# RMSNorm statistics of a two-layer encoder step: plain fp32 averaging and square root with reciprocal, in place of split sums and Ln with Exp

## What is computed

```python
def rms_norm(x, g):
    xf = x.astype(jnp.float32)
    y = xf * lax.rsqrt(jnp.mean(xf * xf, axis=-1, keepdims=True) + EPS)
    return (y * g.astype(jnp.float32)).astype(x.dtype)

for l in range(DEPTH):                                   # DEPTH = 2
    h = rms_norm(xp, ln_mix[l])                          # then projections, attention, x += o @ w_out
    ...
    xp = xp + cross_attend(rms_norm(xp, ln_mem[l]), ...)
    f, cst = conv_ffn(rms_norm(xp, ln_ffn[l]), ...)
    xp = xp + f
y_prompt = rms_norm(xp, ln_final)
```

## Time and profile before

| | us |
|---|---|
| three runs, lowest to highest | 3394.02 to 3395.08 |
| median | 3394.49 |
| the profiled execution | 3398.06 |
| its span in the trace | 3396.3 |

### The profile page before, as it was taken

One profiled execution on the slowest core, in us unless ns is written; L12 is line 12 of the kernel. 1 busy time (PEld: TensorE's weight loads), 2 busy tenths in 40 slices (PEclk: granted clock), 3 DMA queues, 4 the chain that ended last, 5 costly groups with the idle time before them and its releaser, 6 DMA issues.

```text
span 3396.3 us, 50293 instructions
## 1 busy us (share of the span) xinstructions
PE 3238.6 (95%) x20496; PEld 3119.4 (92%) x20496; DVE 1896.0 (56%) x3536; ACT 844.5 (25%) x1960; POOL 1210.1 (36%) x976
## 2 busy tenths in 40 slices
PE   7999999999999999999999999989899999999997
PEld 7888898888899999999988988978889999999997
DVE  6555567676754444444665655576667444444446
ACT  4432333553310000000233333154433000000002
POOL 5213222632443333334342222334424333334331
PEclk9999999999999999999999999999999999999998
DMA  4111222210111111111122112221101111111111
GB/s 159 45 58 45 61 59 68 66 44 29 35 47 45 46 44 44 44 44 47 41 78 58 45 38 64 75 73 48 50 26 44 45 44 44 44 44 47 44 44 64
DMA packets 86021, 177.57 MB, mean 52 GB/s; under 512 B 10544, under 2 KB 13872, under 8 KB 85392
## 3 DMA queue, kind: packets, MB, share of 16 engines
q1 hardware_dynamic: 71968, 132.90, 13.4%
q10 hardware_dynamic: 13824, 41.46, 4.2%
HBM read 150.36 MB, written 16.29 MB: 49 GB/s over the span
## 4 chain that ended last, share of the span: by engine, by line
PE 80%; DVE 11%; ACT 5%; issue 2%; POOL 1%; DMA 0%; SPq 0%; ACTq 0%; DVEq 0%; POOLq 0%
PE PS L611 80%; DVE ACC L1628 2%; ACT PR L1256 1%; DVE HL L1620 1%; DVE PR L1709 1%; DVE XT L1752 1%; ACT PW L1256 1%; DVE PW L1709 1%; DVE XT L1582 1%; ACT PTH L1108 1%; POOL WL L591 1%; DVE PTL L1554 0%; POOL WH L589 0%; DVE DG L1667 0%; ACT G0H L1108 0%
## 5 line engine op out<-in xcount | busy, mean ns | idle before, releaser
L589 POOL TENSOR_TENSOR WH<-RAW,zero 128x512 fp32r<-128x512 f32 x484 | 548.6, 1134 | 2100.7 <-PE PS L611 2086.0
L611 PE MATMUL PS<-HH,WH 128*128 128x384 f32 (+1 forms) x3312 | 865.0, 333 | 43.5 <-DVE HL L1620 17.1
L611 PE MATMUL PS<-HL,WH 128*128 128x384 f32 (+1 forms) x3312 | 849.0, 328 | 0.0
L611 PE MATMUL PS<-HH,WL 128*128 128x384 f32 (+1 forms) x3312 | 849.0, 328 | 0.0
L591 POOL TENSOR_TENSOR WL<-RAW,WH 128x512 fp32r<-128x512 f32 x484 | 666.4, 1377 | 38.0
L611 PEld LDWEIGHTS PS<-HH,WH 128*128 128x128 f32 x3312 | 587.7, 189 | 61.6 <-issue 19.3
L611 PEld LDWEIGHTS PS<-HL,WH 128*128 128x128 f32 x3312 | 590.8, 189 | 0.0
L611 PEld LDWEIGHTS PS<-HH,WL 128*128 128x128 f32 x3312 | 589.7, 188 | 0.0
L1752 DVE TENSOR_TENSOR XT<-PS,XT 128x320 f32<-128x320 f32 x464 | 314.1, 718 | 264.7 <-PE PS L611 264.5
L611 PE MATMUL PS<-G0H,WH 128*128 128x384 f32 (+1 forms) x960 | 275.4, 339 | 25.4 <-DVE XT L1582 16.6
L1108 ACT ACTIVATE PTH<-PS 128x512 fp32r<-128x512 f32 (+4 forms) x320 | 165.4, 520 | 530.8 <-PE PS L611 529.5
(11 more groups left out here) (255 smaller groups left out, 4715.9 us busy)
## 6 DMA issues: line engine op xcount, KB each, us to landing
RAW<-in_slabs SPq DMA_DIRECT2D x484, 256.0 KB, 2.6
XR<-decays ACTq DMA_DIRECT2D x16, 512.0 KB, 5.8
XT<-in_xT SPq DMA_DIRECT2D x8, 544.0 KB, 8.4
out_fk<-T ACTq DMA_DIRECT2D x8, 544.0 KB, 2.7
XR<-decays ACTq DMA_DIRECT2D x16, 272.0 KB, 7.0
out_fv<-T ACTq DMA_DIRECT2D x8, 544.0 KB, 2.8
out_y<-YT ACTq DMA_DIRECT2D x8, 544.0 KB, 3.2
RX<-ST ACTq DMA_DIRECT2D x24, 136.0 KB, 4.0
```

The lines of the kernel that those rows point to most:

```text
L589: pool.tensor_tensor(WH[:, s, :], RAW[:, s, :], zero[:, 0:1].to_broadcast([128, HALF]), ALU.add).then_inc(w_hi, 1)
L611: ins = pe.matmul(*a, **k)
```

## The change

All seven norms change in the same way, on three engines:

- Nobody splits the sums. `stat` waits for the last `sq_used`, and multiplies `ACC` itself with `mean`, the same 128 x 128 tile read as fp32: three matmuls with fp32 operands in place of six with fp32r.
- ScalarE (`rms`): two Sqrt, 768 and 320 columns, each with a count of `rms_ready`. No Exp over 1088.
- VectorE (`invert_rms`): a reciprocal in place over 768 columns after the first count, one over 320 after the second.
- `exp_table` is new: an Exp of one column, thrown away. It stands behind the Sqrt of the mix and memory norms, and behind the Ln of the forget gates. The mixer norm and the final one have none.

```diff
-                pe.wait_ge(stat_ready, place.at("norm", 1))
+                pe.wait_ge(sq_used, place.at("norm", KT - 1, KT - 1))
                 pe.wait_ge(g_free, place.at("group", 2))
                 pe.wait_ge(o_free, place.at("step", 1))
-                for k, x in enumerate((SH, SL)):
-                    for (a, b), o in zip(CH, STAT):
-                        mm(pe, PS[:, o:o + b - a], mean_r[:], x[:, a:b], start=k == 0, stop=k == 1)
+                for (a, b), o in zip(CH, STAT):
+                    mm(pe, PS[:, o:o + b - a], mean, ACC[:, a:b], start=True, stop=True)
...
-            def split_sums(act):
-                act.wait_ge(sq_used, place.at("norm", KT - 1, KT - 1))
-                hi(act, [(SH[:], ACC[:])])
-
-            def inverse_rms(act):
+            def rms(act):
                 act.wait_ge(stat_done, place.at("norm", 1))
                 act.activation(like(R, 0, 768), PS[:, STAT[0]:STAT[0] + 1024].rearrange("p (c n) -> p c n", c=2)[:, :, 0:384],
-                               ACT.Ln, bias=eps[:])
-                wait_own(act, act.activation(R[:, 768:T], PS[:, STAT[2]:STAT[2] + T - 768], ACT.Ln, bias=eps[:]))
-                act.activation(R[:], R[:], ACT.Exp, scale=-0.5).then_inc(rms_ready, 1)
+                               ACT.Sqrt, bias=eps[:]).then_inc(rms_ready, 1)
+                act.activation(R[:, 768:T], PS[:, STAT[2]:STAT[2] + T - 768], ACT.Sqrt, bias=eps[:]).then_inc(rms_ready, 1)
                 place.add("norm")
+
+            def exp_table(act):
+                act.activation(SM[:, 0, 0:1], one[:], ACT.Exp)
...
-            def split_sums(dve):
-                lo(dve, [(SL[:], ACC[:], SH[:])]).then_inc(stat_ready, 1)
-
-            def await_rms(dve):
+            def invert_rms(dve):
+                dve.wait_ge(rms_ready, place.at("norm", 1, 2))
+                dve.reciprocal(R[:, 0:768], R[:, 0:768])
+                dve.wait_ge(rms_ready, place.at("norm", 2, 2))
+                wait_own(dve, dve.reciprocal(R[:, 768:T], R[:, 768:T]))
                 place.add("norm")
-                dve.wait_ge(rms_ready, place.at("norm"))
```

More of the change, by code:

```diff
@@ L201, in encoder_step @@
         mean_r = sb("mean_r", [128, 128], F32R)
+        mean = mean_r[:].bitcast(F32)
         causal_r = sb("causal_r", [128, 128], F32R)
@@ L240, in encoder_step @@
         SQ = [t[:] for t in SQ]
-        SH, SL = QH, QL
         MSQ = here("MSQ", [128, KT, MEM], F32, PT0)
@@ L317, in encoder_step @@
         msq_ready, msq_used, mstat_ready, rm_ready = (sem(n) for n in ("msq_ready", "msq_used", "mstat_ready", "rm_ready"))
-        stat_ready, stat_done, rms_ready, attn_ready = (sem(n) for n in ("stat_ready", "stat_done", "rms_ready", "attn_ready"))
+        stat_done, rms_ready, attn_ready = (sem(n) for n in ("stat_done", "rms_ready", "attn_ready"))
         h_ready = sem("h_ready")
@@ L1282, in down @@
                     place.add("third")
-                if gains is not None or last:
-                    split_sums(act)
             def rope_swap(act, base, k):
@@ L1298, in _ @@
                 residual(act0, kt, LC[0][:, C_MIX:C_MIX + KT], SQ)
-            split_sums(act0)
             def layer(act, l):
@@ L1304, in layer @@
                 act.dma_start(CLF[:], clogf[l]).then_inc(clf_in, 16)
-                inverse_rms(act)
+                rms(act)
+                exp_table(act)
                 filled(act)
@@ L1513, in _ @@
                 layer(act0, l)
-            inverse_rms(act0)
+            rms(act0)
             for kt in range(KT):
@@ L1772, in down @@
                     add_squares(dve, KT - 1, KT - 1)
-                if gains is not None or last:
-                    split_sums(dve)
             def rope(dve, base, k, nth, out):
@@ L1802, in _ @@
             add_squares(dve0, KT - 1, KT - 1)
-            split_sums(dve0)
             masks(dve0)
@@ L1807, in layer @@
                 LC[0] = LCS[:, l, :]
-                await_rms(dve)
+                invert_rms(dve)
                 wait_full(dve, place)
@@ L1984, in _ @@
                 layer(dve0, l)
-            await_rms(dve0)
+            invert_rms(dve0)
             for kt in range(KT):
```

## The result

The changed kernel is slower: 3430.88 us, median of 5 runs (3422.27 to 3435.55), against 3394.49 of the kernel before beside it (5 runs, 3394.01 to 3406.67). The ratio is 1.0093, with a 95% interval of 1.0073 to 1.0113. The forecast of 3380.5 had the wrong sign. The profiled run took 3435.55, with a span of 3433.8, which is 37.5 more than the profiled run before.

The account below looks back on a forecast made before the run. TensorE, busy 95%, was taken to bound the kernel. Memory and layer 1 mix norms -4.6, mixer norms -5.4, first mix norm +0.6, final norm -2.2, attention -2.6 made -14.2 us: 3383.9 profiled, 3380.5 as median; range 3373 to 3394.

Parts of the forecast that it names:

- The split goes: Ahead of each norm's average: without split sums TensorE no longer stands; layer 0's memory-norm average ends 1.19 us earlier, fp32 included.
- The average in fp32: At each norm's average on TensorE: fp32 matmuls run as two instructions each and take 1.9 us, +0.9 a norm.
- The inverse: After each norm's average: ScalarE's Sqrt takes what Ln took, then VectorE's two wide reciprocals cost 1.4 us together.
- r = 1.4: Time in us of both VectorE reciprocals of a norm, taken at the TensorTensor's 1.02 ns a column.
- The bound of 3.5: Upper estimate in us for a norm's two reciprocals: 3 ns a column over 1088 columns, with the fixed part.
- What is late next: Behind layer 0's memory-norm average: TensorE's own work is last, 1.1 us to spare, going on 1.54 earlier; no gain at r = 4.0.
- the sum: Gains by place over all norms and the first attention steps, -14.2 us together, with TensorE going on 1.54 earlier at memory norms.
- more if the clock falls after each stand: Addition to the slow wide reciprocal's 3428: further loss if TensorE's clock drops after waits at the norms; no size given.
- The first attention's table load: First attention step of each layer: moving the 1.28 us load brings value copies earlier, -2.6 in all; TensorE's stand near 0.8.
- a slow wide reciprocal: Rival, chance 0.18: at the norms VectorE's reciprocal takes eight steps a column, r = 9.2, holding TensorE; 3428 us or more.
- The second column adds 3 ns, where eight steps would add 8: Argument against the slow wide reciprocal, from softmax reciprocals of one column (156 ns) and two (159 ns).
- The second rival: Chance 0.12: gain eaten, within 0.2%, by reciprocals at 3 ns a column, clock and value copies, or GpSimd's weights; 3393 together.

Follow-up runs that it names:

- experiment 5: The changed kernel with a multiplication of the same width in place of each reciprocal (outputs not the reference's): 3383.2 us, ratio 0.9963; the unaltered changed kernel beside it: 3426.81.
- experiment 1: The changed kernel with the inverse by Ln and Exp as before and no throwaway Exps, so only the fp32 average is new: 3383.84 us, ratio 0.9971.
- experiment 3: The kernel before with reciprocals of 1 to 320 columns added at its end, each followed by a TensorTensor of the same width: 6.25 ns a column from 32 to 128.
- the repeat: The changed kernel run again, unaltered against its first measurement, beside later variants: 3426.81 us, ratio 1.0092 of the kernel before.

## Why the prediction was wrong

Its steps in turn:

- **The split goes: right.** TensorE's stand of 1.8 ahead of the average is gone at every norm that has projections behind it. With a cheap inverse, or with Ln and Exp, nothing else takes its place. The clock at the mixer norm comes back with it: 0.57 in the earlier trace rows, 1.00 in experiment 5. The gains of the norms, taken place by place there, are within 0.3 of the forecast.
- **The average in fp32: right.** It was put at 1.9 and costs 1.83, so +0.8 a norm in place of +0.9. The start of the next pair after 1.59 hides 0.24 of it, and the expectation of experiment 1, which took 1.59, was that much too hopeful: -1.3 a norm was measured where it had -1.4, and -2.2 at the mixer norms where it had -2.5. The number of instructions was right: the trace shows six for the three matmuls. At the final norm, after a stand, the six take 3.8, as forecast.
- **The inverse: wrong. This is the step that failed.** "From above: reciprocals of one column take 156 ns, of two 159; 3 ns a column over 1088 is 3.3, with the fixed part 3.5. I take the TensorTensor's rate, r = 1.4, as the nearest". The two rows are right and the slope between them is not the rate: columns cost 3 and 9 ns in turn (experiment 3), 6.25 on average. The bound of 3.5 was thus no bound, and the value taken was below it without any row on a wide reciprocal. The TensorTensor was near in its width and far in its operation; the narrow reciprocal was the right operation, seen at one step. r is 7.0.
- **What is late next: right as a rule.** "At r = 4.0 the gain is nil": with 7.0, three microseconds past that, memory norms lost. Put r = 7.0 in its own line, and TensorE goes on at 759.67 + 7.0 + 0.54 = 767.2, 4.5 later than in the sum; measured are stands of 4.34 to 4.48. The final norm loses 5.6 more than forecast: 6.3 + 5.6 = 11.9 against a measured 11.8.
- **The sum with the right r.** Six times 4.5 and 5.6 are 32.6, which on 3382 (experiment 5) gives 3415. By the ratios, 1.0093 and 1.0092 of 3394.49, the changed kernel takes 3426, 11 more. The prediction had named what is missing, "more if the clock falls after each stand", and not priced it. It is measured: against the same matmuls in experiment 1, where nothing stands, those behind the six stands lose 1.4, 1.5, 2.0, 2.7, 1.6 and 2.2 us in the first profile, 11.4 in all, and 12.2 in the repeat's. With them the sum is 3426 to 3427. The medians as they stand, 3431 and 3427, leave up to 5 us, which is within the spread of the runs; what sets the stretches at the lower clock in the attentions was not separated.
- **The first attention's table load: right,** within what a timeline tells. The stands with the load moved are 1.41 and 1.37 in one profile and 1.18 and 0.80 in the other, where 0.8 was forecast.
- **The rivals.** The first, a slow wide reciprocal, was what happened, at a chance of 0.18. Its 3428 was nearly the measured time, partly for the wrong reason: it had eight steps a column, r = 9.2, and left the clock without a price. The real case has six steps and the clock's fall. "The second column adds 3 ns, where eight steps would add 8" was the argument against it, and it was worth much less than it seemed: one difference between two neighbouring sizes can't tell a rate from a rhythm. The second rival, that the gain is eaten elsewhere, did not happen.

The Trainium skill ("VectorE: DVE Perf Modes", First, the fixed hardware budget) with its repeat count of 8 pointed to the right side; the trace has 6.25 ns a column where eight steps of 1.04 would be 8.3. What the Trainium skill ("Vector Engine (DVE) Microarchitecture Reference", 3.2 Anatomy of a single slice) says of a chain over all eight slices, which I had read as allowing one step, gives no rate.

As to the chances: two statements stood against each other on a term that only a wide instruction could settle, and the break-even was within a factor of three of the value taken. 0.18 for the bad side was too little for that, and without it the range ended at 3394.

## What to carry to other kernels

In these runs a column of a reciprocal on VectorE costs six times that of a multiplication, 6.25 ns against 1.04; at 320 columns the whole instruction takes 2132 ns against 422. It is nothing for the one or two columns of a softmax row sum, and 7 us for a statistic spread over 1088 columns; to use it there, first count its columns and then look at what VectorE owes TensorE at that moment. ScalarE's Ln and Exp, with a table load between them, take 3.7 us for the same and leave VectorE free. When an operation occurs in the trace only at sizes that differ by one, take no rate from it; a microbenchmark of a few widths at the end of the kernel costs one run.

## What the runs showed of the hardware that I had not expected

- The reciprocal's steps of 3 and 9 ns for odd and even columns (152, 155, 164, 167 ns for 1 to 4 columns, each of one instruction), and 6.25 ns a column from 32 columns on.
- A stand of TensorE costs more than its length. Behind stands of 4.3 to 4.5 us the matmuls ran at half speed for some 3 to 6 us, and 1.4 to 2.7 were lost each time; behind 1.81 us at the mixer norm the clock fell too, while behind 1.82 at layer 0's memory norm the pairs kept their step.
- The clock also is low with TensorE busy: 0.50 from 1775 to 1795 in the changed kernel's profile, with no idle time; the last stand ahead of it was one of 1.37 that ended at 1769. The same kernel shows 0.58 in one profile and 0.83 in the next over the same forty microseconds, and the kernel before has 0.57 in layer 0's first attention. What makes the stretch long or short stays open: no run separated it.
